# The dilated branch of a hybrid decoder layer: the first head's probabilities transposed by VectorE in 32x32 squares and moved through HBM

## What is computed

```python
C_GROUPS = ((128, 1), (512, 4), (2048, 16))          # (window, dilation)
# for each group, per block of 128 queries:
logits = einsum('bqhd,bqjhd->bhqj', qb, ks) * scale - slopes * dist
logits = where(valid, logits, -inf)
lse = logsumexp(logits, axis=-1)
p = exp(logits - lse[..., None])
o = einsum('bhqj,bqjhd->bqhd', p, vs)
# then, over the groups at each position and head slot:
alpha = softmax(stack(lses), axis=0)                  # weights of the group outputs
y = x + (sigmoid(ga)*(ya @ w_a) + sigmoid(gb)*(yb @ w_b) + sigmoid(gc)*(yc @ w_c)) @ w_o
```

## Time and profile before

| | before |
|---|---|
| median of 3 runs | 1376.3 us (1376.18 to 1376.54) |
| profiled execution | 1376.36 us |
| its span | 1374.6 us |
| granted TensorE clock | 0.999 of full speed |
| busy: TensorE / VectorE / ScalarE / GpSimd | 98% / 54% / 48% / 11% |
| instructions | 20906 |
| DMA | 114.37 MB in 114677 packets |

### The profile page before, as it was taken

The page is one execution under the profiler, slowest core; times in us unless marked ns, Lnnn a source line. Parts: engine busy times, 40 slices in busy tenths (PEclk is TensorE's granted clock), DMA queues, the critical chain, the costliest instruction groups (busy, mean ns, idle before and its releaser), DMA issues.

```text
span 1374.6 us, 20906 instructions
## 1 busy us (share of the span) xinstructions
PE 1352.1 (98%) x7882; PEld 1102.6 (80%) x7882; DVE 741.4 (54%) x1675; ACT 659.3 (48%) x1430; POOL 153.2 (11%) x259
## 2 busy tenths in 40 slices
PE   7999999999999999999999999999999999999998
PEld 6988877777878888887878777787888788888886
DVE  6568866666757874574434455533333354222634
ACT  7467766666644531115454565645454422113223
POOL 3123111102112000001101012100000030000100
PEclk9999999999999999999999999999999999999999
DMA  6055222212224322323303032211322242231522
GB/s 222 24 138 131 66 66 62 69 40 64 70 50 125 88 72 67 84 90 98 93 24 93 24 101 90 66 47 55 108 62 62 62 149 67 78 84 62 185 89 102
DMA packets 114677, 114.37 MB, mean 83 GB/s; under 512 B 10609, under 2 KB 96049, under 8 KB 114321
## 3 DMA queue, kind: packets, MB, share of 16 engines
q1 hardware_dynamic: 97824, 58.22, 15.7%
q0 software_dynamic: 16752, 54.82, 12.6%
HBM read 87.37 MB, written 21.45 MB: 79 GB/s over the span
## 4 chain that ended last, share of the span: by engine, by line
PE 92%; DVE 4%; ACT 2%; issue 1%; POOL 1%; DMA 0%; POOLq 0%; ACTq 0%; DVEq 0%
PE bank L1053 22%; PE bank L1055 22%; PE bank L1054 22%; PE bank L1199 6%; PE bank L1220 6%; PE slot L1187 6%; PE slot L1053 2%; PE slot L1054 2%; PE slot L1055 2%; DVE idle_out L1586 1%; PE slot L1161 1%; DVE slot L1771 1%; DVE qc L1714 1%; PE bank L1066 0%; ACT qc L1412 0%
## 5 line engine op out<-in xcount | busy, mean ns | idle before, releaser
L1053 PE MATMUL bank<-hs,w_hl 128*128 128x512 f32 x1088 | 431.8, 397 | 3.8 <-DVE qc L1714 2.9
L1055 PE MATMUL bank<-hs,w_hl 128*128 128x512 f32 x1088 | 424.3, 390 | 0.0
L1054 PE MATMUL bank<-hs,w_hl 128*128 128x512 f32 x1088 | 423.8, 390 | 0.0
L1053 PEld LDWEIGHTS bank<-hs,w_hl 128*128 128x128 f32 x1088 | 204.3, 188 | 48.9 <-issue 8.5
L1559 DVE TENSOR_TENSOR w_hl<-w_raw,w_hl 128x512 fp32r<-128x512 f32 (+1 forms) x168 | 113.5, 678 | 235.7 <-ACT w_hl L1284 234.1
L1055 PEld LDWEIGHTS bank<-hs,w_hl 128*128 128x128 f32 x1088 | 204.1, 188 | 43.6
L1054 PEld LDWEIGHTS bank<-hs,w_hl 128*128 128x128 f32 x1088 | 204.6, 188 | 39.6
L1284 ACT ACTIVATE w_hl<-w_raw 128x512 fp32r<-128x512 f32 (+1 forms) x168 | 103.9, 621 | 161.6 <-PE bank L1055 154.1
L1586 DVE TENSOR_SCALAR_CACHE_REDUCE idle_out<-score,state 128x768 uint8<-128x768 f32 (+3 forms) x140 | 115.3, 824 | 4.8
L1771 DVE CUSTOM_DVE_ANT_0 slot<-slot,score 128x128 f32<-128x128 f32 (+5 forms) x64 | 47.0, 786 | 75.4 <-PE slot L1187 75.4
L1468 ACT ACTIVATE idle_out<-score,state 128x896 bf16<-128x896 f32 x64 | 70.0, 1093 | 10.0 <-DVE state L1582 8.8
(11 more groups left out here) (320 smaller groups left out, 2211.2 us busy)
## 6 DMA issues: line engine op xcount, KB each, us to landing
w_raw<-in_w_in_dram SPq DMA_DIRECT2D x136, 256.0 KB, 2.9
merged_scratch<-ms POOLq DMA_DIRECT2D x16, 512.0 KB, 3.5
ms<-merged_scratch POOLq DMA_DIRECT2D x16, 512.0 KB, 3.8
xn<-in_x_dram SPq DMA_DIRECT2D x8, 512.0 KB, 6.8
iq_st<-iq_hl POOLq DMA_DIRECT2D x32, 128.0 KB, 2.8
w_raw<-in_w_o_dram SPq DMA_DIRECT2D x16, 256.0 KB, 3.7
v_scratch<-vtc POOLq DMA_DIRECT2D x6, 512.0 KB, 3.0
vc<-v_scratch POOLq DMA_DIRECT2D x24, 128.0 KB, 3.8
```

Of the source, the lines that this page charges most:

```text
L1053: pe.matmul(out_, wh, mh, start=start, stop=False)
L1054: pe.matmul(out_, wh, ml, start=False, stop=False)
L1055: return pe.matmul(out_, wl, mh, start=False, stop=stop)
```

## The change

For branch c, all runs but the last (23 of 24), the first head takes another way; the second head stays as it was.

- A new step `square` stands between `pv` and `turn`. ScalarE makes the first head's exponentials there. VectorE transposes them in place in 32x32 squares (up to 512 columns). GpSimd's queue stores the result in HBM (one of two scratch tensors in turns), waits for the store, and issues four loads that put the squares in their places in PTQ (two buffers).
- ScalarE waits with the exponentials of a run for the store of the run before, since both use row 0 of PR["c"]. GpSimd waits before the loads for the product of the run two before.
- `turn` and `exp` do the second head alone, so a run has one group of transposes, of 4, 3 or 2 blocks. The ring of turned groups is 2 for branch c.
- TensorE waits before the product of a run for its four loads.

```diff
+SQUARED = ("c", )
+LAG = {"c": 2, "a": 3, "b": 2}
-PTS = 4
+PTS = {"c": 2, "a": 4, "b": 4}
...
+        by_dma = [r[0]["br"] in SQUARED and s + 1 < n and (r[0]["br"] == "c" or r[0]["ch"] + 1 < NCH["a"])
+                  for s, r in enumerate(runs)]
...
-            if s >= 2:
+            late = LAG[runs[0][0]["br"]]
+            due = [r for r in range(max(s - 3, 0), min(s, n)) if r + (late if by_dma[r] else 2) == s]
+            for r in due:
                 pv = ring()
...
+            if s < n and by_dma[s]:
+                step("square", unit=runs[s][-1], n=len(squares), before=squares[-2] if len(squares) > 1 else None)
...
-                parts = [(x["b"], hh, c) for x in runs[s - 1] for hh in range(2) for c in range(x["W"] // P)]
+                parts = [(x["b"], hh, c) for x in runs[s - 1] for hh in range(1 if x["dma"] else 0, 2)
+                         for c in range(x["W"] // P)]
...
+        PTQ = {"c": [at(k, f"ptsc{k}", [P, 4, P]) for k in (58, 60)]}
...
+                elif kind == "square":
+                    u, n, mid = a["unit"], a["n"], square_dram[a["n"] % 2]
+                    br, W = u["br"], u["col"] + u["W"]
+                    pool.wait_ge(squared, n + 1)
+                    if n >= 2:
+                        pool.wait_ge(square_in, 64 * (n - 1))
+                    pool.dma_start(mid[0:W // P].rearrange("b p c -> p b c"),
+                                   PR[br][:, 0, 0:W].rearrange("p (b c) -> p b c", c=P)).then_inc(square_stored, 16)
+                    if a["before"] is not None:
+                        full(pool, a["before"]["pv"])
+                    pool.wait_ge(square_stored, 16 * (n + 1))
+                    for j in range(4):
+                        pool.dma_start(PTQ[br][n % 2][32 * j:32 * j + 32, 0:W // P, :].rearrange("a b (i c) -> a (b i) c", i=4),
+                                       mid[0:W // P, :, 32 * j:32 * j + 32].rearrange("b (i a) c -> a (b i) c", i=4)
+                                       ).then_inc(square_in, 16)
...
+                        if a["dma"]:
+                            pe.wait_ge(square_in, 64 * (a["square"] + 1))
...
+                elif kind == "square":
+                    u = a["unit"]
+                    if a["n"]:
+                        act.wait_ge(square_stored, 16 * a["n"])
+                    act.wait_ge(logit_ready, u["L"][0] + 1)
+                    for x in u["run"]:
+                        mx, dn = stats_of(x, 0)
+                        ins = A(PR[x["br"]][:, 0, x["col"]:x["col"] + x["W"]], slot_of(x, 0)[1], ACTF.Exp, bias=mx,
+                                scale=-1.0, accum_out=dn)
+                    ins.then_inc(slot_free if u["slots"] == 2 else single_exp, 1)
...
+                elif kind == "square":
+                    u = a["unit"]
+                    W = u["col"] + u["W"]
+                    if u["slots"] == 2:
+                        dve.wait_ge(slot_free, u["S"] + 1)
+                    else:
+                        dve.wait_ge(single_exp, u["single"] + 1)
+                    v.transpose(PR[u["br"]][:, 0, 0:W], PR[u["br"]][:, 0, 0:W]).then_inc(squared, 1)
```

More of the change, by code:

```diff
@@ L223, in pair_run @@
         n = len(runs)
+        by_dma = [r[0]["br"] in SQUARED and s + 1 < n and (r[0]["br"] == "c" or r[0]["ch"] + 1 < NCH["a"])
+                  for s, r in enumerate(runs)]
+        for run, dma in zip(runs, by_dma):
+            for x in run:
+                x["dma"] = dma
         defer[0] = True
@@ L243, in turn @@
                 step("turn", unit=run[0], groups=groups)
-            between = 1 <= s < n and runs[s - 1][0]["slots"] == 2
+            between = 1 <= s < n and runs[s - 1][0]["slots"] == 2 and not by_dma[s - 1]
             if s < n and not between:
                 logits()
-            if s >= 2:
+            late = LAG[runs[0][0]["br"]]
+            due = [r for r in range(max(s - 3, 0), min(s, n)) if r + (late if by_dma[r] else 2) == s]
+            for r in due:
                 pv = ring()
-                for x in runs[s - 2]:
+                for x in runs[r]:
                     x["pv"] = pv
                     plan.append(("pv", x))
+            if s < n and by_dma[s]:
+                step("square", unit=runs[s][-1], n=len(squares), before=squares[-2] if len(squares) > 1 else None)
+                for x in runs[s]:
+                    x.update(square=len(squares), single=sum(y["slots"] == 1 for y in squares))
+                squares.append(runs[s][-1])
             if 1 <= s <= n:
-                parts = [(x["b"], hh, c) for x in runs[s - 1] for hh in range(2) for c in range(x["W"] // P)]
+                parts = [(x["b"], hh, c) for x in runs[s - 1] for hh in range(1 if x["dma"] else 0, 2)
+                         for c in range(x["W"] // P)]
                 groups = [dict(parts=parts[g0:g0 + 4]) for g0 in range(0, len(parts), 4)]
@@ L677, in hybrid_layer_kernel @@
         v_stored, v_in = sem("v_stored"), sem("v_in")
+        single_exp, squared, square_stored, square_in = sem("single_exp"), sem("squared"), sem("square_stored"), sem("square_in")
+        square_dram = [nc.dram_tensor(f"square_scratch_{i}", [TB, P, P], F32, kind="Internal").ap() for i in range(2)]
         v_dram = [nc.dram_tensor(f"v_scratch_{i}", [P, T], F32, kind="Internal").ap() for i in range(2)]
@@ L816, in turned_room @@
         def turned_room(eng, grp):
-            if grp["tp"] >= PTS:
-                full(eng, info["unit_of_tp"][grp["tp"] - PTS]["pv"])
+            ring = PTS[info["unit_of_tp"][grp["tp"]]["br"]]
+            if grp["tp"] >= ring:
+                full(eng, info["unit_of_tp"][grp["tp"] - ring]["pv"])
         block = ctx.enter_context(nc.Block())
@@ L1213, in _ @@
                         first = a["b"] // 2 * 2
-                    at_part = {part: (grp["tp"] % PTS, j) for grp in a["groups"] for j, part in enumerate(grp["parts"])}
+                    at_part = {part: (grp["tp"] % PTS[a["br"]], j) for grp in a["groups"] for j, part in enumerate(grp["parts"])}
                     for c in range(n):
                         for hh in range(2):
-                            t, j = at_part[a["b"], hh, c]
+                            if a["dma"] and hh == 0:
+                                turned = PTQ[a["br"]][a["square"] % 2][:, a["col"] // P + c, :]
+                            else:
+                                t, j = at_part[a["b"], hh, c]
+                                turned = PT[a["br"]][:, t, j, :]
                             cols = slice(HD * hh, HD * hh + HD)
                             values = V["b"][:, c, :] if a["br"] == "b" else V[a["br"]][a["ch"] % 2][:, first + c, cols]
-                            ins = pe.matmul(bank[a["pv"][0]][cols, out], values, PT[a["br"]][:, t, j, :],
+                            ins = pe.matmul(bank[a["pv"][0]][cols, out], values, turned,
                                             start=c == 0, stop=c == n - 1)
@@ L1429, in _ @@
                         full(act, a["held"]["groups"][-1]["use"])
-                    for hh in range(2):
+                        if a["held"]["dma"] and not a["dma"]:
+                            act.wait_ge(square_stored, 16 * (a["held"]["square"] + 1))
+                    for hh in range(1 if a["dma"] else 0, 2):
                         act.wait_ge(logit_ready, a["L"][hh] + 1)
@@ L1444, in _ @@
                         turned_room(act, grp)
-                        A(PT[u["br"]][:, grp["tp"] % PTS, 0:n, :].rearrange("p c q -> p (c q)"), bank[b][:, 0:n * P],
+                        A(PT[u["br"]][:, grp["tp"] % PTS[u["br"]], 0:n, :].rearrange("p c q -> p (c q)"), bank[b][:, 0:n * P],
                           ACTF.Copy).then_inc(bank_free[b], 1)
```

5 lines of the change are left out of this document (3 added, 2 removed).

## The result

The changed kernel takes 1401.84 us (median, 1398.85 to 1403.24) against 1376.35 us: ratio 1.0182, 95% interval 1.0163 to 1.0202. The forecast was 1387.5 with a range of 1375.5 to 1394. The sign was right, the size was not. The profiled execution took 1403.24 us, with a span of 1401.5 and a mean granted clock of 0.989. It is one of the two longest of four: the others took 1398.85 and 1400.44 us at a mean clock of 0.991.

The account below looks back on a forecast made before the run. VectorE's in-order queue was taken to pace TensorE in nine steps. Saved 5.3 us against 10.35 (late bits) + 4.75 (last channel) + 1.3 (first channel) = 16.4: net 11.1 on 1376.36, so 1387.5 us, range 1375.5 to 1394.

Parts of the forecast that it names:

- What it removes: First head's 68 of 140 TensorE transposes go; 5.3 us saved in the steps where TensorE doesn't wait.
- steps B and C: Steps where TensorE waits for VectorE's evacuation of q or k, eight in all; removed transposes save nothing there.
- Delay of the bit: VectorE's new transpose delays the threshold bit (small operations, four counts): 4.0 us over B, 6.35 over C, together 10.35.
- The store behind the v move: First and last channel: a run's store queues on GpSimd behind v's store, wait and four loads; 1.3 and 4.75 us.
- step 21: Last channel's step where TensorE already waits; exponentials wait for the late store, bit at 366.65 for 361.89, 4.75 us.
- The loads: Four loads per run on GpSimd's queue: 3.7 us to land in the first channel, otherwise hidden with some 22 us.
- the rival at 1500 us: Transposing loads slow in themselves: at 20 us each, some 20 steps would grow by 6; chance 0.02.
- the granted clock stays at full: In the dilated branch's stretch, 136 to 396 us, clock 1.00 (2.4 GHz); no clock step charged.
- First channel: Late store and loads behind the v move; the fifth step starts 1.3 us later than before.
- Other channels: "hidden, with 2.2 us in hand": Stores behind v moves in the other channels land about 2.2 us before the exponentials are ready; charged nothing.
- GpSimd becomes the bound: Rival: slowest landings use up the 2.2 us margin in four channels, both waits grow by 2; 1395 us, chance 0.08.

Follow-up runs that it names:

- e1: Kernel before, with the first head's 68 transposes left out and nothing in their place (part of the output left out): 1369.25 us, ratio 0.995.
- e7: Kernel before, nothing moved, with two 512-column and two 256-column extra VectorE transposes ahead of each threshold bit: 1412.54 us, ratio 1.0264.
- e3: Changed kernel without the store and four loads; early exponentials and VectorE transposes stay, part of the output left out: 1385.89 us, ratio 1.0070.
- e5: As e4, with VectorE's transpose, the store and the loads moved to the end of the step: 1373.97 us, ratio 0.9981.
- e9: As e5, with the first run's first head left to TensorE: 1370.97 us, ratio 0.9962.
- run 0: Not an experiment: the first of the dilated branch's 24 runs inside the kernel, one step of the plan each; no time of its own.
- e2: Kernel before, nothing moved, with one 512-column and one 256-column extra VectorE transpose ahead of each threshold bit: 1389.15 us, ratio 1.0096.
- e6: As e5, but with the changed kernel's one row for the first head's probabilities: 1393.61 us, ratio 1.0119.
- e10: As e9, with ScalarE's early exponentials also ahead of the output copy: 1370.71 us, ratio 0.9960.
- e4: Changed kernel with two rows used in turns, so exponentials wait for the store of the run before the last: 1390.03 us, ratio 1.0096.

## Why the prediction was right in sign and wrong in size

**Right.** *What it removes*: the transposes went 0.97 to 0.41, 1.00 to 0.30 and 0.41 to 0.20 us per step, as written; the steps that keep the saving gave 5.1 for 5.3; e1 confirms both the 6.9 us in all and that steps B and C keep none of it. The 275 ns of the Trainium skill, TensorE: Matmul & The Clock Gate, section PE-mode transpose, would have made 18.7 us of the 68, for the 11 of all steps together; the start-to-start rows were the right price. *Delay of the bit*: 1.16 for 1.15 in the first B. VectorE's SBUF transpose took 0.71, 0.58 and 0.445 us at 512, 384 and 256 columns; I had 0.72, 0.54 and 0.36. Over B and C the steps grew by 12.0, but 2.8 of that are store waits; VectorE's lateness was 9.2 for 10.35, near 4.0 in B and 1.2 too large in C. *The store behind the v move*: the right queue and the right two places; step 21 lost 5.2 for 4.75. *The loads*: 1.9, 2.2, 4.8 us to land (min, median, max), so the rival at 1500 us was far off. The Trainium skill, VectorE: DVE Perf Modes, section The three transpose paths, warns of a plain strided copy 19 times slower than the crossbar transpose when the innermost destination stride is large; these loads move contiguous pieces of 128 bytes and no run here has a crossbar transpose, so the ratio itself was not put to the test. GpSimd's busy time was never the bound, its order was.

**The step that failed**: "the granted clock stays at full (1.00, the 2.4 GHz level), so no clock step enters the sum". That was read from before, where the longest wait of TensorE in the branch was about 1 us. My own terms then made waits of some 2 us in eight steps and of over 4 in one more, and I kept the clock. Half clock cost 11.6 of the 27.1 us of the profiled execution. Without it that execution would have taken about 1391.6 us (1403.24 less 11.6), inside the range. e7 and e3 show that it follows from the waits and needs no transfer; the traces of e5 and e9, which do all or nearly all of the same work with one wait of 2.2 us or none that long, have none. The other terms were 4.4 us too small in sum (15.5 for 11.1), and that alone would not have left the range.

**Terms that were too small**:

- *First channel*, 1.3 us, was 3.4. The store landed 5.8 us after its issue (145.15 to 150.97) where I took 3.15 from the v stores: it went out while the v loads were still in flight, the last of which landed at 150.7. Its lateness of 1.7 went through VectorE's queue as I had it, and the evacuation of k came 2.2 us behind TensorE in step 3 instead of 0.4. TensorE's wait for the loads was then only 0.8, for 2.4.
- *A tenth late step*, missing from the list and a part of these 3.4 us: step 1. The transpose of run 0 delays its bit, the evacuation of q comes behind that, and TensorE waits 1.6 us after its transposes (143.6 to 145.21). The step grew by 1.3 where it was to shrink by 0.33. e2 has it too (11.44).
- *Other channels: "hidden, with 2.2 us in hand"*, put at nothing, was 2.8. In two of four it was not hidden: step 13 waited 2.4 us for a store that took 6.7 us to land, step 17 1.4 (the rest of the 14.2 us) for one that took 6.1. The margin was worked out from one channel and one landing time, though the rival "GpSimd becomes the bound" named just this. Two of the four places went its way; I gave it 0.08.

Landing times were taken from rows in which the queue carried less. The DMA share rose from 0.23 to 0.33, and the store's slowest landing was 6.7 us against 3.9 for the v move's. All six slow stores were those behind a v move, so the place behind the loads marks them; that the higher share had a part in it is not shown.

**What stays open**: what decides whether a wait is followed by half clock. In the changed kernel waits of 2.47, 2.08, 4.37, 2.11, 1.97 and 5.66 us inside the blocks were, waits of 2.11, 2.08 and 3.02 (steps 9, 10, 17) were not; in e7 3.35, 2.74, 3.10, 3.15, 3.55 and 3.44 were, 2.44, 2.50 and 3.03 were not; in e2 none up to 2.32 was, in e3 2.44, 2.08 and 2.12 were and 2.45, 2.23, 2.10 and 2.09 were not, in e6 3.17 was not. Below 1.9 us none was in any run. Length alone does not sort them, and no run here was made to find what does. Nor is the number of stretches fixed by the kernel: four executions of the changed kernel had mean clocks of 0.988 to 0.991 and times 4.4 us apart, so the 11.6 us belong to the profiled one (0.989), and the two at 0.991 had less. Nor did I follow up the 0.5 us that step 21 keeps in e5 and e9 but not in e10.

## What to carry to other kernels

An engine that is busy half the time can still set the pace, if the buffers of the busy one are freed by instructions that stand in its in-order queue: find those, and put new work behind them, not ahead (16 us here for the same instructions, e4 against e5), with a second buffer to pay for the longer life of the data. Where a change adds waits to TensorE of about 2 us or more, count on some of them being followed by half clock even if the profile of before shows full clock throughout, and widen the range for it. Compare the mean clock of the traced execution with that of the others: one trace is one draw (e5). A DMA whose landing is on the path should be priced behind what is in flight at that moment, not by the median of another transfer.

## What the runs showed of the hardware that I had not expected

- Half clock came in stretches of 3.4 us, or twice that at the longest waits of the changed kernel (4.37 and 5.66 us) and at two of e6 (3.1 and 3.9 us), and cost up to 1.6 us per single stretch: matmuls of 512 columns 0.427 us apart instead of 0.227. So a wait of 2.1 us, once followed by it, costs about 3.7.
- VectorE's in-place SBUF transpose of 512 fp32 columns took 711 ns in the changed kernel and 699 to 711 in e2, hardly less than the 716 ns from PSUM.
- A store of 256 KB or less from GpSimd's queue landed 2.2 to 2.7 us after its issue, and 4.6 to 6.7 us when it was issued while a v move's loads were in flight; a quarter of it, loaded in pieces of 128 bytes, in 2.2 us in the median.
